# Differential heads of a transformer kernel: one bias product opens each score bank, then the scores of both components in turn

## The reference, cut to what matters

```python
q = q.reshape(b, s, h, 2, HEAD_DIM_2).transpose(0, 2, 1, 3, 4)   # h = 8, two components of 64
k = k.reshape(b, s, h, 2, HEAD_DIM_2).transpose(0, 2, 1, 3, 4)
slopes = alibi_slopes(h)                                         # 2 ** -(head + 1)
...
    sc = jnp.einsum('bhqcd,bhkcd->bhcqk', q_blk, k) * scale
    dist = jnp.abs(q_pos[:, None] - k_pos[None, :])
    bias = -slopes[:, None, None] * dist
    allowed = k_chunk[None, :] <= (q_pos // CHUNK)[:, None]
    sc = jnp.where(allowed, sc + bias[None, :, None], -jnp.inf)
    p = jax.nn.softmax(sc, axis=-1)
    w = p[:, :, 0] - lam * p[:, :, 1]
    return jnp.einsum('bhqk,bhkv->bhqv', w, v)
```

## Time and profile before

| | us |
|---|---|
| three runs | 2159.2, 2159.2, 2156.79 (median 2159.2) |
| the profiled execution | 2157.39 |
| its span, first to last instruction | 2155.6 |
| TensorE busy in it | 2092.7 (97%) |
| VectorE / ScalarE / GpSimdE busy | 1456.3 / 996.9 / 570.1 |
| mean granted TensorE clock | 0.994 |
| stage of the differential heads | about 1188 to 1310 |

### The profile page before, as it was taken

The page is one execution under the profiler, slowest core; times in us unless marked ns, Lnnn a source line. Parts: engine busy times, 40 slices in busy tenths (PEclk is TensorE's granted clock), DMA queues, the critical chain, the costliest instruction groups (busy, mean ns, idle before and its releaser), DMA issues.

```text
span 2155.6 us, 29543 instructions
## 1 busy us (share of the span) xinstructions
PE 2092.7 (97%) x11646; PEld 1775.3 (82%) x11646; DVE 1456.3 (68%) x1984; ACT 996.9 (46%) x1428; POOL 570.1 (26%) x551
## 2 busy tenths in 40 slices
PE   7999999999899999989999999999999999999997
PEld 6788888887788888778877788788888888888886
DVE  8866776667666556757655667677776557777755
ACT  5545444444532554433445454454444334444443
POOL 8215542233300244691121222301100000111122
PEclk9999999999999999999999999999999999999999
DMA  7554665655654433565554435555666665666664
GB/s 247 181 185 149 188 188 185 186 178 186 195 179 133 131 105 118 158 200 167 159 163 137 137 128 162 171 185 188 186 186 184 187 191 185 183 192 186 178 185 135
DMA packets 104091, 370.01 MB, mean 172 GB/s; under 512 B 11633, under 2 KB 12945, under 8 KB 103825
## 3 DMA queue, kind: packets, MB, share of 16 engines
q1 hardware_dynamic: 103952, 368.13, 54.8%
HBM read 365.98 MB, written 2.10 MB: 171 GB/s over the span
## 4 chain that ended last, share of the span: by engine, by line
PE 84%; POOL 6%; DVE 5%; issue 2%; ACT 2%; DMA 0%; DVEq 0%; SPq 0%; POOLq 0%; ACTq 0%
PE psg L508 46%; PE psg L510 22%; POOL s_zf L2358 2%; DVE s_wl L1580 2%; PE psg L555 2%; PE psg L557 2%; PE psg L556 2%; PE psg L507 1%; PE pst L508 1%; ACT s_wh L1065 1%; POOL s_acc L2534 1%; POOL s_psq L2282 1%; POOL s_psq L2527 1%; PE pst L592 1%; DVE s_rh L1598 1%
## 5 line engine op out<-in xcount | busy, mean ns | idle before, releaser
L1580 DVE TENSOR_TENSOR s_wl<-s_stage,s_wh 128x1024 fp32r<-128x1024 f32 (+3 forms) x699 | 869.8, 1246 | 391.5 <-ACT s_wh L1065 389.0
L1065 ACT ACTIVATE s_wh<-s_stage 128x1024 fp32r<-128x1024 f32 (+3 forms) x699 | 725.8, 1041 | 673.4 <-PE psg L508 361.6
L508 PE MATMUL psg<-s_ry,s_wh 128*128 128x512 f32 x2672 | 946.5, 401 | 3.4 <-DVE s_mv L1647 2.5
L510 PE MATMUL psg<-s_ry,s_wl 128*128 128x256 f32 x2501 | 703.3, 281 | 0.0
L508 PEld LDWEIGHTS psg<-s_ry,s_wh 128*128 128x128 f32 x2672 | 493.7, 188 | 119.1 <-issue 6.7
L508 PE MATMUL psg<-s_rh,s_wh 128*128 128x512 f32 x1280 | 461.9, 405 | 19.2 <-DVE s_rh L1598 9.2
L510 PEld LDWEIGHTS psg<-s_ry,s_wl 128*128 128x128 f32 x2501 | 473.1, 189 | 7.2
L510 PE MATMUL psg<-s_rh,s_wl 128*128 128x256 f32 x1180 | 332.1, 281 | 0.0
L508 PEld LDWEIGHTS psg<-s_rh,s_wh 128*128 128x128 f32 x1280 | 238.1, 189 | 79.5 <-issue 13.0
L508 PE MATMUL psg<-s_hid,s_wh 128*128 128x512 f32 x704 | 245.9, 399 | 0.0
L510 PEld LDWEIGHTS psg<-s_rh,s_wl 128*128 128x128 f32 x1180 | 224.2, 190 | 2.8
(11 more groups left out here) (393 smaller groups left out, 2340.9 us busy)
## 6 DMA issues: line engine op xcount, KB each, us to landing
s_stage<-in_wo SPq DMA_DIRECT2D x96, 512.0 KB, 3.5
s_stage<-in_wg SPq DMA_DIRECT2D x88, 512.0 KB, 3.5
s_stage<-in_wu SPq DMA_DIRECT2D x88, 512.0 KB, 3.6
s_stage<-in_ain SPq DMA_DIRECT2D x64, 512.0 KB, 3.5
s_stage<-in_wd SPq DMA_DIRECT2D x64, 448.0 KB, 3.4
s_stage<-in_wkv SPq DMA_DIRECT2D x32, 512.0 KB, 3.7
s_stage<-in_wd SPq DMA_DIRECT2D x32, 512.0 KB, 3.6
s_stage<-in_bq SPq DMA_DIRECT2D x24, 512.0 KB, 3.6
```

The costliest lines, as they stand in the source:

```text
L508: m = e.matmul(o, M.WH[:, r, ws], xx, start=begin, stop=end)
L510: m = e.matmul(o[:, T:2 * T], M.WL[:, r, ws], xh, start=False, stop=False)
L1065: e.activation(M.WH[:, c % NR, 0:n], M.ST[:, c % NS, 0:n], ACT.Copy).then_inc(S["wh"], 1)
L1580: e.tensor_tensor(M.WL[:, c % NR, 0:n], M.ST[:, c % NS, 0:n], M.WH[:, c % NR, 0:n], ALU.subtract).then_inc(S["wl"], 1)
```

## The change

The four bias products of a head become two, one per bank, each over all 384 columns, and they come first, with start=True. The four score products follow with start=False. They are ordered by segment, and within a segment by component. The waits before and the semaphore after are the same.

```diff
         w.wait_ge("ddb", 1)
         for c in range(2):
-            rows = slice(64 * c, 64 * c + 64)
-            s = M.PSS[:, c, :]
-            e.matmul(s[:, 0:128], qa[rows, 0, 0:128], qa[rows, 1, 0:128], start=True, stop=False)
-            e.matmul(s[:, 0:128], M.IDS[:, h, :], M.DDB[:, 0:128], start=False, stop=True)
-            e.matmul(s[:, 128:384], qa[rows, 0, 128:256], qa[rows, 1, :], start=True, stop=False)
-            m = e.matmul(s[:, 128:384], M.IDS[:, h, :], M.DDB[:, 128:384], start=False, stop=True)
+            e.matmul(M.PSS[:, c, 0:384], M.IDS[:, h, :], M.DDB[:, :], start=True, stop=False)
+        for q, (a, b) in enumerate(CSEG):
+            for c in range(2):
+                rows = slice(64 * c, 64 * c + 64)
+                m = e.matmul(M.PSS[:, c, a:b], qa[rows, 0, 128 * q:128 * q + 128], qa[rows, 1, 0:b - a], start=False, stop=q == 1)
         m.then_inc(S["l2_s"], 1)
```

## The result

| | before | after |
|---|---|---|
| median of four runs, us | 2157.99 (2156.7 to 2159.2) | 2145.68 (2145.14 to 2147.04) |
| profiled execution, us | 2157.39 | 2145.21 |
| its span, us | 2155.6 | 2143.4 |

The ratio is 0.9944, 95% interval 0.9932 to 0.9955, so between 9.7 and 14.7 us less. The forecast was 2146.8 and the gain 11.5 us; two later comparisons of the same two kernels gave 0.9939 (0.9923 to 0.9956) and 0.9941 (0.9929 to 0.9953). By their medians the three gains are 12.3, 13.1 and 13.1 us; all three intervals hold 11.5 as well.

What follows compares the result with a forecast made beforehand. TensorE was taken to bound the differential heads. Biases 0.44 plus scores 1.19 make 1.63 us a head against 3.07, saving 11.5 us over eight heads: 2146.8 us, the middle of two bases, range 2144.2 to 2150.5.

Steps and rivals of the forecast that it cites:

- TensorE bounds the stage, and the saving reaches the end: Differential heads: TensorE is busy for all of a 15.5 us period, so its savings reach the end unless new waits arise.
- 3.07 us a head before, 1.63 after: TensorE's time per differential head: 0.44 + 1.19 = 1.63 us against 3.07, saving 1.44 a head, 11.5 for eight.
- bias term: Two 384-column biases per head: 0.17 us, then 0.27 with the change to 64 rows, together 0.44; bounds 0.34 to 0.54.
- score term: Eight score passes per head overlap on both array halves: 1.19 us with the way back, taken from the band attention heads.
- The changes of the array's mode: TensorE in the old head: about 0.10 us going from full array to 64 rows, about 0.20 coming back.
- The level: Whole kernel's end time: 2146.8 us, the middle of 2145.9 (from the profiled execution) and 2147.7 (from the median).
- VectorE's cover: Low half of weights behind the maxima, for the second unit after the scores: cover shrinks from 0.71 to 0.36 us, no wait.
- the 1.86 and 0.42 of the first unit: First weight unit after the scores: its weights' cover shrinks from 1.86 to 0.42 us.
- Rival 2: VectorE's maxima or splits slip past the 0.36 us cover, TensorE waits once a head: 3.5 us given back, 2150.3; chance 0.10.
- Program order: Rival 1: score passes on the two halves overlap only in program order, 0.21 us a head more, 2148.5; chance 0.12.
- No overlap: Rival 3: accumulating halves run one after the other, 0.64 us a head more, gain only 6.4, 2151.9; chance 0.06.
- a drain of every pass: Rival 4: each score pass waits for the one before to finish, 3.8 us a head against 3.07, 2164; chance 0.02.

Runs made afterwards that it cites:

- split experiments: Against the changed kernel: each merged bias right before its component's scores, 2152.57 us; or the four old biases, two behind each segment's paired scores, 2147.55 us.
- run with biases alone: The changed kernel with the four score products left out, so the softmax sees only the biases: 2137.36 us, ratio 0.9906 to the kernel before.
- scores-first run: The changed kernel with the four scores opening the banks and the two merged biases last: 2144.86 us, ratio 0.9936; in five rounds 2145.62 us, 0.9941.

## Why the prediction was right, and where it was not

**TensorE bounds the stage, and the saving reaches the end.** Right: 11.60 us in the stage, and what follows it unchanged to less than 0.1 us. The run with four more products a head and the one without scores moved the end as far as TensorE's own time: +5.5 us in the stage and 2151.34 at the end, -8.7 us and 2137.36.

**3.07 us a head before, 1.63 after.** Right to 0.01 us. The bias term came out at 0.42 for 0.44, the score term at 1.20 for 1.19. Taking the score term whole from the chunk-band heads was what made it exact: it brought the way back at L508 with it, which is 0.1 us dearer than the 0.20 read from the earlier trace rows. Those rows aren't from the differential heads' own stage, as the prediction has it, but from 1051 us; TensorE was as busy there, at the same granted clock:

```profile
1045.00:1060.00 15.00, 15.00 (x91) 12.19 (x91) 9.69 (x15) 8.92 (x18) 0.53 (x1) 1.00 0.42 142
```

The changed heads have the same eight passes, and adding onto an open bank cost nothing, as the earlier trace rows had suggested. Eight times 1.44 is 11.5; the stage shows 1.45 a head.

**The changes of the array's mode.** The 0.10 us to the half array and the 0.20 back, read out of the earlier trace rows, carried the forecasts of the split experiments (2.58 for 2.57 measured, 1.81 to 1.86 for 1.83). The 0.20 holds for the way back to a bias; back to L508 it was about 0.30.

**The level.** Forecast 2146.8, measured 2145.68. The gain was right; the base was the middle between the profiled execution's time and a median of three, 2159.2, that a fourth run brought to 2157.99. From that, 11.5 us less is 2146.5.

**VectorE's cover: the step that failed.** The maxima did lose their wait of 1.09 us, as said; VectorE takes them at 1218.17 with no idle time. But "0.71 us of cover before, 0.36 us after" was misread, and so was the 1.86 and 0.42 of the first unit. In the changed kernel, VectorE in order of time:

```profile
1210.06 1.23 DVE L1579 TENSOR_TENSOR s_wl<-s_stage,s_wh 128x1024 fp32r<-128x1024 f32 x1 [3.82 <-ACT s_wh L1064]
...
1212.61 1.22 DVE L1579 TENSOR_TENSOR s_wl<-s_stage,s_wh 128x1024 fp32r<-128x1024 f32 x1
...
1215.97 1.22 DVE L1579 TENSOR_TENSOR s_wl<-s_stage,s_wh 128x1024 fp32r<-128x1024 f32 x1
...
1218.17 0.42 DVE L1754 TENSOR_REDUCE s_stat<-pss 128x2 f32<-128x256 f32 x1
1218.50 0.68 DVE L1755 TENSOR_REDUCE s_stat<-pss 128x2 f32<-128x512 f32 x1
1219.10 1.21 DVE L1579 TENSOR_TENSOR s_wl<-s_stage,s_wh 128x1024 fp32r<-128x1024 f32 x1
```

and the units on TensorE:

```profile
1213.24 0.58 PE L508 MATMUL psg<-s_ry,s_wh 128*128 128x512 f32 x1
...
1217.50 0.50 PE L508 MATMUL psg<-s_ry,s_wh 128*128 128x512 f32 x1
...
1220.68 0.48 PE L508 MATMUL psg<-s_ry,s_wh 128*128 128x512 f32 x1
...
1224.17 0.48 PE L508 MATMUL psg<-s_ry,s_wh 128*128 128x512 f32 x1
```

Each unit uses the low part that is one earlier than the prediction took. The n-th L1579 belongs to the n-th unit, since both programs go through the 699 units in the same order. So the unit at 1217.50 uses the low part that was ready at 1213.83 (3.7 us of cover), the one at 1220.68 that of 1217.19 (3.5), and the one at 1224.17 that of 1220.31 behind the maxima (3.9). In the kernel before, that last low part was ready at 1225.00 and its unit started here, with 4.2 us of cover:

```profile
1229.19 0.48 PE L508 MATMUL psg<-s_ry,s_wh 128*128 128x512 f32 x1
```

So the loss of about 0.35 us was forecast rightly; the level it is taken from was wrong by a whole unit. The thinnest cover is that of the unit at 1213.24, whose low part is ready at 1211.29 (1210.06 + 1.23): 2.0 us. That low part waits for ScalarE (the 3.82 in its row), and ScalarE first takes the transposes and then four exponentials, ahead of its next copy at 1208.95:

```profile
1206.98 0.49 ACT L1375 ACTIVATE s_cpt<-pst 128x384 f32<-128x384 f32 x1 [3.38 <-PE pst L907]
```

It hangs on the transposes, not on the scores, so its cover did not shrink: the same count gives 2.0 in the kernel before, and 1.9 to 2.0 in the run with biases alone. The forecast did not suffer, since it took "enough for no wait" either way. Rival 2 and its chance of 0.10 did: they rested on 0.36 us where the real cover behind the maxima is 3.9 and the thinnest anywhere in the stage's periods is 2.0.

**The other rivals.** Program order (0.12) is out by the scores written component by component, which cost 0.01 us a head. No overlap (0.06) and a drain of every pass (0.02) are out by the eight passes in 0.85 us.

## What to carry to other kernels

Products on 64 rows of the two halves of TensorE's array ran at once when no full-array product stood between them, in whatever order they were written; so look for full-array products between small ones and move them to one side. What counted was how often they interrupt the small ones, and their columns, not how many products they are. Every change between full and half array cost 0.1 us going and 0.2 to 0.3 coming back here, more than a short bias product's own columns. To price such a change, find a stretch of the same kernel that already has the wanted sequence and take its time whole. Before calling a margin thin, count which buffer a step fills: with three buffers, the part that ends just before a unit need not be that unit's.

## What the runs showed of the hardware that was not expected

- Coming back to the full array cost more than leaving it, and how much depended on what came first there: about 0.2 us at a bfloat16 bias, about 0.3 at the weight product L508. The forecast of the scores-first run had the total of 1.52, but nothing had been said of this: it is the 0.1 us a head between 1.52 with the biases behind the scores and 1.62 with them ahead. Why L508 pays more is open.
- Forecast from the rows, but shown only here: four passes of one component and eight of both take the same 0.86 us up to the next full-array product, so the second half came free: 0.85 to 0.86 in both written orders.
- Also forecast: two 384-column bfloat16 products and four of 128 and 256 columns take the same 0.43 us up to the first score, though each of the four has its own weight load.
